# FOX heads of a hybrid attention block: weighing by three products of split operands, transposes in one row

## The chip, the cores and the metric

The kernel runs on one core of one Trainium2 chip. The metric is the device time of one execution in microseconds; three runs were taken and the median stands for the kernel.

## The reference, cut to what matters

One decoder layer in float32, 512 tokens, model width 2048: RMSNorm, one combined projection, native sparse attention (8 heads, the NSA part), forgetting attention (8 heads of 128, the FOX part), a gated merge of both, an output projection, and a feed-forward block with a depthwise convolution. The change touches the FOX part alone:

```python
def fox_attention(q, k, v, f_logit, f_bias):
    log_f = jax.nn.log_sigmoid(f_logit + f_bias)
    cum = lax.cumsum(log_f, axis=1).transpose(0, 2, 1)
    ...
    logits = einsum('bqhd,bkhd->bhqk', qblk, k) * scale + (cq[..., None] - cum[:, :, None, :])
    p = masked_softmax(logits, kpos[None, :] <= tpos[:, None])
    o = einsum('bhqk,bkhd->bqhd', p.astype(v.dtype), v)
```

## The kernel before, in words

Every engine has its own program written out by hand; semaphores order them. Large products are made of operands split into a high part rounded to fp32r and a low part that is the rest: `three` (its products are L809 to L811) issues high x high, high x low and low x high into one accumulation. Small products use plain float32, which the profile records as two passes.

The stage between the two halves of the merge holds the eight FOX heads, 0 to 7. TensorE's part of one head is `fox_step` on the tensor engine (L1175): scores of four query tiles (3, 2, 0, 1) into banks 2 to 4, split for all but tile 0; then products of a filler, `slot_cols`, which is one of the 22 plain blocks of the combined projection (16 steps `k` of three products of 512 columns, L809 to L811), there so that TensorE has work while the softmax of the head runs on VectorE (DVE) and ScalarE (ACT); then four transposes of V from `vf_fm` into bank 4 (L1187), ten transposes of the probabilities `l_fox` (L1085), the last filler step, and the weighing (`weigh`, L1091): O = V^T P^T with `vf_tm` as the stationary operand and `pt_f` as the moving one, for key tiles 0, 1, 3, 2 over 512, 384, 128 and 256 columns, into bank 7. The stage ends with one more filler block and `merge(S_BB, 1)`.

In each head DVE adds the bias and takes the maximum (L2207), splits the next filler's weights (`w_lo`, L1923), scales the probabilities (L2320), splits the next head's q and k (`fox_lo`, L2302), copies one bank of transposed probabilities to `pt_f` (L2326), and writes the filler's output (`plain_out`, L2152). ACT makes `w_hi` (L1361), issues the DMAs of the next head's `q_f` and `k_f` (L1645), takes the exponentials (L1564), rounds the next head's q and k (`fox_hi`, L1635), copies bank 4 to `vf_tm` (L1651), and banks of transposed probabilities to `pt_f` (L1653, L1655), and bank 7 to `y32` (L1657). Both run strictly in this order, so whatever waits for `q_f` and `k_f` holds up the copies behind it. SyncE (SP) issues per head, in this order: `vf_fm` of the next head (L675), the store of a filler's output (L593), `bias_f` (L679) and the weights of a later filler (`w_raw`, L499). POOL's queue meanwhile makes sums of feed-forward weights in DRAM.

## Time and profile before

| what | value |
|---|---|
| median of 3 runs | 2674.88 us (2674.46 to 2674.95) |
| profiled execution | 2675.92 us, its span 2674.1 us |
| FOX heads in the profile | scores of head 0 at about 940 us, weighing of head 7 to 1075.6 us |
| length of one head without a stall | 16.90 us |
| granted TensorE clock, mean | 0.995 |

PE is TensorE's matmuls, PEld its weight loads. A matmul's duration in the profile runs past the start of the next one, since they are pipelined: what an instruction costs is the distance from its start to the start of the next. SPq and ACTq are the issue of DMAs on those engines. Heads are counted from 0.

### The profile page before, as it was taken

To read this page: it belongs to the slowest core of one execution; us is meant where nothing else is said; L and a number is where in the kernel's file an instruction comes from. 1 tells how busy PE (TensorE), PEld (TensorE's weight loads), DVE (VectorE), ACT (ScalarE), POOL (GpSimd) and SP (SyncE) were. 2 spreads that over 40 slices of the span, in tenths; PEclk is the share of its full clock that TensorE was granted. 3 is DMA by queue.
4 is the path that set the end of the run, shared out by engine and by line. 5 is a ranking of instruction groups with operands and counts; after the bars stand their busy time and mean duration, and the time that the engine had idled before them with its cause. 6 is when DMAs were issued, how large, how long until landed. Compare 5 with 4: busy or idle time off the path is not lost.

```text
span 2674.1 us, 39866 instructions
## 1 busy us (share of the span) xinstructions
PE 2637.6 (99%) x14729; PEld 2280.2 (85%) x14729; DVE 2016.6 (75%) x2565; ACT 1227.7 (46%) x1618; POOL 497.4 (19%) x354
## 2 busy tenths in 40 slices
PE   8999999999999999999999999999999999999998
PEld 6899999987888877888888999999999998888886
DVE  5899899875554354542289999999999998888876
ACT  6444444434444244422355555555555544444445
POOL 0144444441442121220001111000000000000002
PEclk9999999999999999999999999999999999999999
DMA  7565666666666589779628888744354446666664
GB/s 224 148 194 176 196 181 177 200 191 172 158 165 177 175 248 254 236 242 247 183 87 212 208 193 208 157 126 122 106 133 114 107 114 234 223 229 224 221 210 151
DMA packets 499163, 489.54 MB, mean 183 GB/s; under 512 B 11589, under 2 KB 376790, under 8 KB 498281
## 3 DMA queue, kind: packets, MB, share of 16 engines
q1 hardware_dynamic: 454855, 367.14, 46.2%
q0 software_dynamic: 36112, 106.36, 16.5%
q10 hardware_dynamic: 8114, 14.95, 1.6%
q8 instruction: 50, 0.82, 0.1%
q14 instruction: 32, 0.26, 0.0%
HBM read 425.46 MB, written 127.96 MB: 207 GB/s over the span
## 4 chain that ended last, share of the span: by engine, by line
PE 92%; DMA 3%; DVE 2%; ACT 2%; issue 1%; SPq 0%; ACTq 0%; POOL 0%; DVEq 0%
PE bank L859 23%; PE bank L868 14%; PE bank L1343 14%; PE bank L861 12%; PE bank L809 8%; PE bank L811 8%; PE bank L810 8%; PE bank L1091 2%; PE bank L1085 1%; DMA k_f<-p_dram 1%; DMA w_raw<-in_w_in_dram 1%; DMA d_raw<-in_w_down_dram 1%; DVE ring_lo L2367 0%; DMA w_raw<-in_cmp_w_v_dram 0%; ACT sq_junk L1393 0%
## 5 line engine op out<-in xcount | busy, mean ns | idle before, releaser
L859 PE MATMUL bank<-hl,ring_hi 128*128 128x512 f32 x1032 | 368.4, 398 | 0.5 <-ACT v_sb L1735 0.5
L1343 PE MATMUL bank<-fold_hi,y_slot 128*128 128x512 f32 x1120 | 345.0, 389 | 0.0
L861 PE MATMUL bank<-hl,ring_lo 128*128 128x256 f32 x1032 | 289.8, 281 | 0.0
L1343 PEld LDWEIGHTS bank<-fold_hi,y_slot 128*128 128x128 f32 x1120 | 210.2, 188 | 43.8
L1923 DVE TENSOR_TENSOR w_lo<-w_raw,w_hi 128x2048 fp32r<-128x2048 f32 x59 | 135.9, 2303 | 145.6 <-ACT w_hi L1361 145.6
L1831 ACT ACTIVATE fold_hi<-x_raw 128x1024 fp32r<-128x1024 f32 x140 | 148.5, 1063 | 201.5 <-PE bank L1343 199.4
L859 PEld LDWEIGHTS bank<-hl,ring_hi 128*128 128x128 f32 x1032 | 194.0, 188 | 46.9 <-ACT v_sb L1735 0.7
L2771 POOL TENSOR_TENSOR v_sb<-v_sb,conv_t 128x512 f32<-128x512 f32 x44 | 68.3, 1552 | 881.2 <-ACT conv_t L1749 867.8
L1711 ACT ACTIVATE ring_hi<-s_a 128x1024 fp32r<-128x1024 f32 x129 | 137.0, 1062 | 202.7 <-PE bank L861 104.1
L1343 PE MATMUL bank<-fold_lo,y_slot 128*128 128x512 f32 x560 | 217.8, 389 | 0.0
L859 PE MATMUL bank<-hl,q_ring_hi 128*128 128x512 f32 x600 | 214.3, 399 | 2.3 <-issue 1.8
L861 PEld LDWEIGHTS bank<-hl,ring_lo 128*128 128x128 f32 x1032 | 195.1, 189 | 0.0
L2546 DVE TENSOR_TENSOR fold_lo<-x_raw,fold_hi 128x1024 fp32r<-128x1024 f32 x140 | 172.1, 1230 | 24.3 <-ACT fold_hi L1831 24.3
L809 PE MATMUL bank<-hl,w_hi 128*128 128x512 f32 x448 | 182.1, 407 | 6.4 <-DVE w_lo L1933 3.2
L1361 ACT ACTIVATE w_hi<-w_raw 128x2048 fp32r<-128x2048 f32 x59 | 113.0, 1915 | 163.5 <-PE bank L811 144.0
L811 PE MATMUL bank<-hl,w_lo 128*128 128x512 f32 x448 | 176.0, 393 | 0.0
L810 PE MATMUL bank<-hl,w_hi 128*128 128x512 f32 x448 | 175.8, 392 | 0.0
L861 PE MATMUL bank<-hl,q_ring_lo 128*128 128x256 f32 x600 | 168.5, 281 | 0.0
L2367 DVE TENSOR_TENSOR ring_lo<-raw,ring_hi 128x1024 fp32r<-128x1024 f32 x129 | 164.0, 1272 | 4.5 <-ACT ring_hi L1711 2.5
L2367 DVE TENSOR_TENSOR ring_lo<-s_a,ring_hi 128x1024 fp32r<-128x1024 f32 x129 | 157.5, 1221 | 5.3 <-ACT ring_hi L1711 5.1
L1423 ACT ACTIVATE q_ring_hi<-q_sum 128x1024 fp32r<-128x1024 f32 x75 | 79.6, 1061 | 161.5 <-DVE q_sum L2028 95.2
L1711 ACT ACTIVATE ring_hi<-raw 128x1024 fp32r<-128x1024 f32 x129 | 136.3, 1057 | 25.1 <-PE bank L868 23.8
(391 smaller groups left out, 7025.2 us busy)
## 6 DMA issues: line engine op xcount, KB each, us to landing
raw<-in_w_up_dram SPq DMA_DIRECT2D x43, 1024.0 KB, 7.2
raw<-in_w_up_dram SPq DMA_DIRECT2D x86, 512.0 KB, 7.5
w_s<-in_w_down_dram POOLq DMA_DIRECT2D x30, 1024.0 KB, 12.6
x_raw<-in_w_down_dram SPq DMA_DIRECT2D x30, 1024.0 KB, 5.1
w_raw<-in_w_in_dram SPq DMA_DIRECT2D x26, 1024.0 KB, 7.6
raw<-in_w_in_dram SPq DMA_DIRECT2D x25, 1024.0 KB, 8.6
raw<-in_w_in_dram SPq DMA_DIRECT2D x50, 512.0 KB, 7.2
x_raw<-w_s SPq DMA_DIRECT2D x20, 1024.0 KB, 5.4
```

The lines of the kernel that those rows point to most:

```text
L809: mm(dst, l_hi, r_hi, start=first, stop=False)
L810: mm(dst, l_hi, r_lo, start=False, stop=False)
L811: return mm(dst, l_lo, r_hi, start=False, stop=final)
L859: mm(pb[bank][:], hi[:, w], high_low(y[0][:, k, :], y[1][:, k, :]), start=first and k == 0, stop=False, skip_group_check=True)
L861: last = mm(pb[bank][:, 0:TH], lo[:, w], y[0][:, k, :], start=False, stop=k == KH - 1, skip_group_check=True)
L868: last = mm(pb[bank][:, 0:TH], left[:, w], y[z][:, k, :], start=first and k == 0 and n == 0, stop=k == KH - 1 and n == 2, skip_group_check ...
L1343: last = mm(pb[banks[tt]][:], y[:, z, k, tk], right[:, w], start=first and k == 0 and m == 0, stop=k == 3 and m == 2, skip_group_check=True)
L1711: A(ring_hi[b][:], src, ACT.Copy).then_inc(piece_hi, 1)
L1831: A(fold_hi[k % RING][:], x_raw[b][:, 1024 * h:1024 * h + 1024], ACT.Copy).then_inc(piece_hi, 1)
L1923: V.tensor_tensor(w_lo[:, s.par, :], w_raw[:, s.par, :], w_hi[:, s.par, :].bitcast(F32), ALU.subtract).then_inc(w_ready, 1)
L2367: V.tensor_tensor(ring_lo[b][:], src, ring_hi[b][:].bitcast(F32), ALU.subtract).then_inc(piece_ok, 1)
L2546: V.tensor_tensor(fold_lo[b][:], x_raw[FOLD_AT[p, n] % 4][:, 1024 * h:1024 * h + 1024], fold_hi[b][:].bitcast(F32), ALU.subtract).then_inc ...
```

## The change

The copies of V and of the transposed probabilities are rounded to fp32r (`vf_tm`, `pt_f`), and DVE makes their low parts: `vf_lo` from bank 4, `pt_lo0` from bank 5 (key tile 0, 512 columns), `pt_lo1` from bank 6 (tiles 1 and 3, 512 columns) and `pt_lo2` from bank 3 (tile 2, 256 columns). The weighing of each key tile is then `three` (products now at L812 to L814) in place of one plain product. The transposes of tile 2 go to bank 3, so that all ten stand in a row, and the filler's last three steps stand behind them in place of one between them and two ahead. `vf_lo` lies where `vf_fm` lies, so SP's load of the next head's V now waits for the end of the weighing (`fpv_done`) and no longer for the transposes of V (`fv_ps`).

```diff
--- before.py
+++ after.py
@@ -289,9 +289,12 @@
     kf_hi = at("kf_hi", A_ + 22 * KB, [P, SEQ], F32R)
     kf_lo = at("kf_lo", A_ + 24 * KB, [P, SEQ], F32R)
     vf_fm = at("vf_fm", A_ + 4 * KB, [P, SEQ])
-    vf_tm = at("vf_tm", A_ + 6 * KB, [P, TOK, P])
+    vf_lo = at("vf_lo", A_ + 4 * KB, [P, TOK, P], F32R)
+    vf_tm = at("vf_tm", A_ + 6 * KB, [P, TOK, P], F32R)
     l_fox = at("l_fox", A_ + 8 * KB, [P, 1280])
-    pt_f = at("pt_f", A_ + 13 * KB, [P, 1280])
+    pt_f = at("pt_f", A_ + 13 * KB, [P, 1280], F32R)
+    pt_lo = [at("pt_lo0", A_ + 26 * KB, [P, 512], F32R), at("pt_lo1", A_ + 32 * KB, [P, 512], F32R), at("pt_lo2", A_ + 34 * KB, [P, 256], F32R)]
+    PT_LO = {0: (0, 0), 1: (1, 0), 3: (1, 384), 2: (2, 0)}
     bias_f = at("bias_f", A_ + 36 * KB, [P, 2, SEQ])
 
     xr = at("xr", A_ + 32 * KB, [P, TOK, 512])
@@ -436,8 +439,8 @@
     f_hi_ok, f_lo_ok = sem("f_hi_ok"), sem("f_lo_ok")
     fs_ready, fs_read, fmax_ready, fexp_done, fr_ready, fp_ready = (
         sem(n) for n in ("fs_ready", "fs_read", "fmax_ready", "fexp_done", "fr_ready", "fp_ready"))
-    fv_ps, fv_ok, ft_ready, ft_act, ft_dve, fpv_done, fo_read = (
-        sem(n) for n in ("fv_ps", "fv_ok", "ft_ready", "ft_act", "ft_dve", "fpv_done", "fo_read"))
+    fv_ps, fv_ok, ft_ready, ft_act, fsplit_ok, fpv_done, fo_read = (
+        sem(n) for n in ("fv_ps", "fv_ok", "ft_ready", "ft_act", "fsplit_ok", "fpv_done", "fo_read"))
     mh_ok, ml_ok = sem("mh_ok"), sem("ml_ok")
     xr_loaded, wo_done, x1_add, x1_sq, x1_put, x1t_ps, x1t_read = (
         sem(n) for n in ("xr_loaded", "wo_done", "x1_add", "x1_sq", "x1_put", "x1t_ps", "x1t_read"))
@@ -671,7 +674,7 @@
 
         def load_fox_v(h):
             if h:
-                sp.wait_ge(fv_ps, h)
+                sp.wait_ge(fpv_done, h + 1)
             sp.dma_start(vf_fm[:], block_in(("VF", h))).then_inc(fv_in, 16)
 
         def load_bias_f(h):
@@ -1090,6 +1093,11 @@
 
             return mm(pb[7][:, j * P:SEQ], v[:, j, :], pt[:, PT_COL[j]:PT_COL[j] + SEQ - j * P], start=first, stop=final)
 
+        def weigh_split(j, first, final):
+
+            n, (b, c) = SEQ - j * P, PT_LO[j]
+            return three(pb[7][:, j * P:SEQ], vf_tm[:, j, :], vf_lo[:, j, :], pt_f[:, PT_COL[j]:PT_COL[j] + n], pt_lo[b][:, c:c + n], first, final)
+
         def nsa_step(s, g, filler):
             pe.wait_ge(q_in, s * 16 + 16)
             pe.wait_ge(o_done, s + 3)
@@ -1180,28 +1188,26 @@
                     pe.wait_ge(fv_ok, h + 1)
                 fox_scores(t).then_inc(fs_ready, 1)
             pe.wait_ge(o_done, h + 12)
-            slot_cols(s, s.par, range(0, KT - 1))
+            slot_cols(s, s.par, range(0, KT - 3))
             pe.wait_ge(fv_in, h * 16 + 16)
             pe.wait_ge(fs_read, h * 4 + 12)
             for j in range(TOK):
                 last = nc.tensor.transpose(pb[4][:, j * P:j * P + P], vf_fm[:, j * P:j * P + P], ident[:])
             last.then_inc(fv_ps, 1)
             pe.wait_ge(fp_ready, h + 1)
-            pe.wait_ge(ft_act, h * 2 + 2)
             transposes([0], 5, l_fox).then_inc(ft_ready, 1)
-            pe.wait_ge(ft_dve, h + 1)
             transposes([1, 3], 6, l_fox).then_inc(ft_ready, 1)
-            slot_cols(s, s.par, [KT - 1])
-            pe.wait_ge(ft_act, h * 2 + 3)
-            transposes([2], 5, l_fox).then_inc(ft_ready, 1)
+            transposes([2], 3, l_fox).then_inc(ft_ready, 1)
+            slot_cols(s, s.par, range(KT - 3, KT))
             pe.wait_ge(fo_read, h + 1)
-            pe.wait_ge(fv_ok, h + 2)
-            weigh(0, vf_tm, pt_f, True, False)
-            pe.wait_ge(ft_dve, h + 2)
-            weigh(1, vf_tm, pt_f, False, False)
-            weigh(3, vf_tm, pt_f, False, False)
-            pe.wait_ge(ft_act, h * 2 + 4)
-            weigh(2, vf_tm, pt_f, False, True).then_inc(fpv_done, 1)
+            pe.wait_ge(fsplit_ok, h * 5 + 1)
+            pe.wait_ge(fsplit_ok, h * 5 + 3)
+            weigh_split(0, True, False)
+            pe.wait_ge(fsplit_ok, h * 5 + 4)
+            weigh_split(1, False, False)
+            weigh_split(3, False, False)
+            pe.wait_ge(fsplit_ok, h * 5 + 5)
+            weigh_split(2, False, True).then_inc(fpv_done, 1)
 
         with pe.Fori(0, 3) as i:
             for b in range(2):
@@ -1652,7 +1658,7 @@
             act.wait_ge(ft_ready, h * 3 + 1)
             A(pt_f[:, 0:512], pb[5][:], ACT.Copy).then_inc(ft_act, 1)
             act.wait_ge(ft_ready, h * 3 + 3)
-            A(pt_f[:, 1024:1280], pb[5][:, 0:256], ACT.Copy).then_inc(ft_act, 1)
+            A(pt_f[:, 1024:1280], pb[3][:, 0:256], ACT.Copy).then_inc(ft_act, 1)
             act.wait_ge(fpv_done, h + 2)
             A(y32[:, ds(h, 1), :].rearrange("p a n -> p (a n)"), pb[7][:], ACT.Copy).then_inc(fo_read, 1)
 
@@ -2321,9 +2327,18 @@
             last.then_inc(fp_ready, 1)
             if more:
                 fox_lo(h + 1)
+            dve.wait_ge(fv_ok, h + 2)
+            dve.wait_ge(fpv_done, h + 1)
+            V.tensor_tensor(vf_lo[:].rearrange("p j d -> p (j d)"), pb[4][:], vf_tm[:].rearrange("p j d -> p (j d)").bitcast(F32),
+                            ALU.subtract).then_inc(fsplit_ok, 1)
             dve.wait_ge(ft_ready, h * 3 + 2)
-            dve.wait_ge(fpv_done, h + 1)
-            V.tensor_copy(pt_f[:, 512:1024], pb[6][:]).then_inc(ft_dve, 1)
+            V.tensor_copy(pt_f[:, 512:1024], pb[6][:]).then_inc(fsplit_ok, 1)
+            dve.wait_ge(ft_act, h * 2 + 3)
+            V.tensor_tensor(pt_lo[0][:], pb[5][:], pt_f[:, 0:512].bitcast(F32), ALU.subtract).then_inc(fsplit_ok, 1)
+            dve.wait_ge(fsplit_ok, h * 5 + 2)
+            V.tensor_tensor(pt_lo[1][:], pb[6][:], pt_f[:, 512:1024].bitcast(F32), ALU.subtract).then_inc(fsplit_ok, 1)
+            dve.wait_ge(ft_act, h * 2 + 4)
+            V.tensor_tensor(pt_lo[2][:], pb[3][:, 0:256], pt_f[:, 1024:1280].bitcast(F32), ALU.subtract).then_inc(fsplit_ok, 1)
             plain_out(1 - b, use + (b + 13) // 2, o_fox[:, 1 - b, :], done.par, done)
 
         with dve.Fori(0, 3) as i:
@@ -2676,7 +2691,7 @@
         pool.dma_start(fb[:], fox_forget_bias.rearrange("a h -> h a")).then_inc(wg_loaded, 16)
 
         for s_, n in ((ns_read, 18), (nt_ready, 6), (nt_dve, 1), (npv_done, 1), (br_read[0], 2), (br_read[1], 2),
-                      (fs_read, 8), (ft_dve, 1), (fpv_done, 1), 
+                      (fs_read, 8), (fpv_done, 1), 
                       (x1t_ps, 1), (x1_sq, 1), (x1_put, 16), (dn_add, 4), (halves_ok, 1), (a_out, 64), (p1_out, 1), (p5_out, 1), (u2_out, 1), (c11_out, 1), (c22_out, 1)):
             pool.sem_inc(s_, n)
```

TensorE, before, from the first transpose of probabilities of head 1 to the first weighing:

```order
L1085 MATMUL bank<-ident,l_fox 128x128 [waits ft_act,fp_ready]
L1085 MATMUL bank<-ident,l_fox 128x128 x3
L1085 MATMUL bank<-ident,l_fox 128x128 [waits ft_dve]
L1085 MATMUL bank<-ident,l_fox 128x128 x3
L809 MATMUL bank<-hl,w_hi 128x512
L810 MATMUL bank<-hl,w_hi 128x512
L811 MATMUL bank<-hl,w_lo 128x512
L1195 REGISTER_ALU
L1085 MATMUL bank<-ident,l_fox 128x128 [waits ft_act]
L1085 MATMUL bank<-ident,l_fox 128x128
L1198 REGISTER_ALU [waits fo_read]
L1091 MATMUL bank<-pt_f,vf_tm 128x512 [waits fv_ok]
```

and the same place now (the filler's three rows come three times):

```order
L1088 MATMUL bank<-ident,l_fox 128x128 [waits fp_ready]
L1088 MATMUL bank<-ident,l_fox 128x128 x9
L812 MATMUL bank<-hl,w_hi 128x512
L813 MATMUL bank<-hl,w_hi 128x512
L814 MATMUL bank<-hl,w_lo 128x512
...
L1203 ISA [waits fo_read]
L1204 REGISTER_ALU [waits fsplit_ok]
L812 MATMUL bank<-pt_f,vf_tm 128x512 [waits fsplit_ok]
L813 MATMUL bank<-pt_lo_110,vf_tm 128x512
L814 MATMUL bank<-pt_f,vf_lo 128x512
```

The ten transposes wait once, nine filler products stand between them and the weighing, and the weighing waits for DVE's splits. On DVE the same head, before, from the split of the next head's k to the next head's logits:

```order
L2302 TENSOR_TENSOR kf_lo<-k_f,kf_hi 128x512 [waits f_hi_ok]
L2324 ISA
L2326 COPY pt_f<-bank 128x512 [waits fpv_done,ft_ready]
L2149 REGISTER_ALU
L2151 ISA [waits w_used]
L2152 TENSOR_TENSOR o_fox<-bank,rbc 128x512 [waits o_put1]
L488 ISA [waits bf_loaded1]
```

and now:

```order
L2308 TENSOR_TENSOR kf_lo<-k_f,kf_hi 128x512 [waits f_hi_ok]
L2330 REGISTER_ALU
L2332 TENSOR_TENSOR vf_lo<-bank,vf_tm 128x512 [waits fpv_done,fv_ok]
L2334 ISA
L2335 CAST pt_f<-bank 128x512 [waits ft_ready]
L2336 ISA
L2337 TENSOR_TENSOR pt_lo_110<-bank,pt_f 128x512 [waits ft_act]
L2338 ISA
L2339 TENSOR_TENSOR pt_lo_111<-bank,pt_f 128x512 [waits fsplit_ok]
L2340 REGISTER_ALU
L2341 TENSOR_TENSOR pt_lo_112<-bank,pt_f 128x256 [waits ft_act]
L2155 REGISTER_ALU
```

Four splits stand around DVE's copy, behind the split of k and ahead of the filler's output.

## Rows read from the trace of the kernel before

**Rows 1.** The page's first part: busy time, share of the span and instructions.

```profile
PE 2637.6 (99%) x14729; PEld 2280.2 (85%) x14729; DVE 2016.6 (75%) x2565; ACT 1227.7 (46%) x1618; POOL 497.4 (19%) x354
```

**Rows 2.** The timeline of TensorE at 971.3 us; columns: start us, us, engine, line, operation.

```profile
971.44 2.32 PE L1091 MATMUL bank<-pt_f,vf_tm 128*128 128x512 f32 x8
...
973.83 0.39 PE L810 MATMUL bank<-kf_lo,qf_hi 128*128 128x512 f32 x1
974.06 0.40 PE L811 MATMUL bank<-kf_hi,qf_lo 128*128 128x512 f32 x1
...
974.60 0.34 PE L810 MATMUL bank<-kf_lo,qf_hi 128*128 128x384 f32 x1
974.77 0.33 PE L811 MATMUL bank<-kf_hi,qf_lo 128*128 128x384 f32 x1
...
975.52 0.28 PE L810 MATMUL bank<-kf_lo,qf_hi 128*128 128x256 f32 x1
975.64 0.28 PE L811 MATMUL bank<-kf_hi,qf_lo 128*128 128x256 f32 x1
```

**Rows 3.** The same view at 985.4 us.

```profile
986.11 0.60 PE L1187 MATMUL bank<-ident,vf_fm 128*128 128x128 f32 x4
986.55 1.04 PE L1085 MATMUL bank<-ident,l_fox 128*128 128x128 f32 x8
```

**Rows 4.** The timeline of all engines, 966.5 to 974 us; brackets: idle before, releaser.

```profile
968.42 0.60 PE L1187 MATMUL bank<-ident,vf_fm 128*128 128x128 f32 x4
...
968.99 0.63 ACT L1635 ACTIVATE qf_hi<-q_f 128x512 fp32r<-128x512 f32 x1 [6.28 <-DMA k_f<-p_dram]
969.05 0.33 SPq L675 DMA_DIRECT2D vf_fm<-p_dram  x1
...
970.87 0.68 DVE L2326 COPY pt_f<-bank 128x512 f32<-128x512 f32 x1
...
971.17 0.44 PE L1085 MATMUL bank<-ident,l_fox 128*128 128x128 f32 x2 [0.58 <-ACT pt_f L1653]
...
971.47 0.68 DVE L2152 TENSOR_TENSOR o_fox<-bank,rbc 128x512 f32<-128x512 f32 x1
```

**Rows 5.** The same view at 1000.2 us, head 3.

```profile
1000.35 0.63 ACT L1635 ACTIVATE qf_hi<-q_f 128x512 fp32r<-128x512 f32 x1 [3.08 <-DMA k_f<-p_dram]
```

**Rows 6.** The same view at 1018.4 us, head 4.

```profile
1018.52 0.63 ACT L1635 ACTIVATE qf_hi<-q_f 128x512 fp32r<-128x512 f32 x1 [4.03 <-DMA k_f<-p_dram]
```

**Rows 7.** The same view at 1035.1 us, head 5.

```profile
1035.24 0.63 ACT L1635 ACTIVATE qf_hi<-q_f 128x512 fp32r<-128x512 f32 x1 [4.04 <-DMA k_f<-p_dram]
...
1036.80 0.27 PE L1187 MATMUL bank<-ident,vf_fm 128*128 128x128 f32 x1
```

**Rows 8.** The same view at 1054 us, head 6.

```profile
1054.12 0.63 ACT L1635 ACTIVATE qf_hi<-q_f 128x512 fp32r<-128x512 f32 x1 [6.19 <-DMA k_f<-p_dram]
...
1056.30 0.44 PE L1085 MATMUL bank<-ident,l_fox 128*128 128x128 f32 x2 [0.43 <-ACT pt_f L1653]
```

**Rows 9.** The tile view of k_f, 934 to 1076 us, its last line.

```profile
DMA to landing us min/median/max: 3.5/6.8/9.1
```

**Rows 10.** The timeline of ACT, 973.5 to 991 us.

```profile
977.57 0.34 ACTq L1645 DMA_DIRECT2D q_f<-p_dram  x1
...
986.75 0.60 ACT L1651 ACTIVATE vf_tm<-bank 128x512 f32<-128x512 f32 x1 [3.56 <-PE bank L1187]
```

**Rows 11.** DMA queues, 959.5 to 969 us: packets, MB, share of 16 engines.

```profile
q0 software_dynamic: 677, 1.62, 74.2%
q1 hardware_dynamic: 942, 0.48, 21.1%
q10 hardware_dynamic: 288, 0.52, 14.6%
```

**Rows 12.** Windows at 587 us: length, busy by engine, PEclk, DMA share, GB/s.

```profile
590.70:594.10 3.40, 3.19 (x8) 2.54 (x9) 0.00 (x0) 1.91 (x1) 0.00 (x0) 0.50 1.15 330
```

**Rows 13.** The timeline of TensorE at 587 us.

```profile
590.91 0.77 PE L809 MATMUL bank<-hl,w_hi 128*128 128x512 f32 x1 [2.96 <-DMA hl<-y_dram]
```

## Prediction

> **What bounds the kernel now.** I read the page first: TensorE is busy 99% of the span, all others 75% or less [rows 1]. So whatever the change saves or adds on TensorE comes out at the end one to one, unless a wait takes it. Next I read TensorE's timeline through the FOX heads. The weighing starts at 971.44; the second product of the scores behind it starts at 973.83, and one product of 512 columns takes 0.23 us, so the weighing truly ends at 973.60 and costs 2.16 us [rows 2]. The filler follows without a gap in most heads. Two heads do stall. In head 1 the last two transposes wait 0.58 us for ACT's copy, in head 6 0.43 us [rows 4, 8]; with the 0.17 us by which a filler product's recorded end runs past its turn, the losses are 0.75 and 0.60 us. The timeline of all engines says why: ACT could begin the next head's qf_hi only when k_f had landed, at 968.99, after 6.28 us of waiting [rows 4], and at 1054.12 after 6.19 us [rows 8]. The copies of V and of the probabilities stand behind that on ACT, and on DVE behind the splits of q and k. So the FOX stage is bound by TensorE with a second limit close beneath: the landing of q_f and k_f, which takes 3.5 to 9.1 us from its issue [rows 9].
>
> **The weighing.** Removed: eight weighings of 2.16 us. Added: per head three products each of 512, 384, 128 and 256 columns. The scores give split products of the same kind: 512 columns 0.23 us (973.83 to 974.06), 384 columns 0.17 us (974.60 to 974.77), 256 columns 0.12 us (975.52 to 975.64) [rows 2]. None of 128 columns is in this trace. Its cost has bounds: by columns alone, half of 256, 0.06 us; and plain float32 at 128 columns, whose one pass is one of the transposes here, (986.55 - 986.11) / 4 = 0.11 us [rows 3], so 0.22 us for both passes. I take 0.12, the split product of 256 columns, since it is the nearest kind and a weight load of 128 columns has to fit into each turn in both. Sum: 3 x (0.23 + 0.17 + 0.12 + 0.12) = 1.92 us, which saves 0.24 us per head, **1.9 us in eight**. The bounds give savings of 3.4 us (0.06) and a loss of 0.5 us (0.22).
>
> The Trainium skill ("TensorE: Matmul & The Clock Gate", section "Back-to-back issue gap") gives about 81 ns for each pair of a weight load and a matmul of 128 columns. By that, an estimate from the page, the three would take 0.24 us in place of 0.36 and the sum would come out 1.0 us lower, at 2676.7; no row here has such a product at full rate.
>
> **The transposes.** They keep their number. Two waits on ACT and one on DVE between them go, worth nothing in the six heads without a stall. The filler keeps its 16 steps. But the first transpose of V now comes two steps earlier, 6 x 0.227 = 1.36 us. Its inputs are ready: l_fox is scaled several us ahead.
>
> **The new wait, and what stands in front of it.** From the first transpose of V TensorE has 14 transposes (14 x 0.109 = 1.53 us) and nine filler products (2.04 us) until the weighing, 3.57 us. The weighing needs DVE's third new step. Head 1 shows the chain, since there all waits for k_f: with A the start of qf_hi, DVE took its copy of pt_f at 970.87 = A + 1.88 and the next instruction 0.60 us later [rows 4]. Now vf_lo stands at A + 1.88, the copy at A + 2.48, the split of tile 0 at A + 3.08, done 0.69 us later; TensorE answers 0.05 us after that, A + 3.82. With T the old start of the transposes of V, TensorE would be there at T - 1.36 + 3.57 = T + 2.21. The stall is A - T + 1.61 where that is positive. The chain from T itself is no limit: vf_tm is written 986.75 + 0.60 - 986.11 = 1.24 us after the first transpose [rows 3, 10], and three DVE steps end 1.9 us later, 0.4 us ahead of TensorE. The later splits (0.60 us apart) end before the 0.69 and 0.85 us of products ahead of them are through.
>
> - Head 1: 968.99 - 968.42 = +0.57, stall 2.18 [rows 4].
> - Head 3: a head without a stall is 16.90 us long, so T is two of them before head 5's: 1000.35 - (1036.80 - 33.80) = -2.65, none, 1.04 to spare [rows 5, 7].
> - Head 4: 1018.52 - (1036.80 - 16.90) = -1.38, stall 0.23 [rows 6, 7].
> - Head 5: 1035.24 - 1036.80 = -1.56, stall 0.05 [rows 7].
> - Head 6: 1054.12 - (1036.80 + 16.90) = +0.42, stall 2.03 [rows 7, 8].
> - Heads 0, 2 have over 4 us to spare, head 7 loads nothing.
>
> Sum 4.5 us, of which 1.35 us was there: **3.1 us added**. In words: the copies have turned into a chain twice as long, and the filler behind the transposes covers it only when k_f is early.
>
> **SP's queue.** The load of V (L675) waited for the transposes of V and was issued at 969.05, 0.63 us after their start [rows 4]; now it waits for the end of the weighing, 3.57 + 1.92 + 0.2 = 5.7 us after the new start, so 3.7 us later. Queued behind it and later by the same: the filler's store, bias_f, and the weights w_raw. Each has a head or more until it is used, so their own lateness costs nothing; if that cover goes, it is w_raw of heads 2 and 7, which would hold ACT's w_hi and with it the exponentials. What matters is that 0.77 MB (three of 256 KB) now flow nearer to q_f and k_f. While these flowed in head 1, they had 0.52 MB in 288 packets, SP's queue only 0.48 MB in 942 small packets, w_raw's, and POOL's 1.62 MB [rows 11]: SP's three loads were over. Bounds of the shift of k_f: nothing or 1 us earlier in head 6, where they overlapped already; at most the whole 0.77 MB ahead of it at the (1.62 + 0.48 + 0.52) MB / 9.5 us = 0.28 MB/us of that stretch, 2.8 us later. I take 0.4 us in each of heads 1, 4, 5 and 6, near the lower end, since V's load now goes out at T + 4.3 and q_f at T + 8.4 (977.57 - 968.42, less the stall of 0.75) [rows 4, 10], so that SP's three should mostly be through: **1.6 us added**.
>
> **Sum.** -1.9 + 3.1 + 1.6 = +2.8 us on 2675.92, the profiled execution's own time, 2678.7. That execution stands 1.04 us above the median of the three runs; on the median it is 2677.7.
>
> **The rivals.**
>
> *Forecast (0.45).* As summed; its own range is 2674.6 (k_f not shifted, 128 columns at 0.06 us) to 2680.1 (k_f 1 us later in four heads).
>
> *Rival 1, slower (0.25): k_f lands later by over 1 us.* SP's three loads and q_f, k_f now share the engines. For it: in head 6 k_f took nearly the 9.1 us, with POOL's and SP's loads in the air. Against it: that lead of some 4 us. From about 1.0 us per head it decides: the result is then slower than before by 0.2%: -1.9 + 3.1 + 4.0 = +5.2. At 1.5 us it is +7.2, 2682.1; at the bound of 2.8 us four heads pay 11.2 and head 3 1.8, and the stall in heads 1 and 6 passes 4.8 us. This trace has an idle stretch of 2.96 us [rows 13] after which TensorE ran 3.4 us at a granted clock of 0.50, 1.2 GHz [rows 12]; at half clock that costs some 1.7 us each, in all +17.6, 2692.5.
>
> The Trainium skill ("DMA: Bandwidth & Descriptors", section "Queues, rings and completion order") says that each DMA engine takes turns between queues packet by packet. By that rule SP's large packets would get as many turns as q_f's where w_raw's small ones took little. By that rule the trace agrees: small packets moved few bytes each (0.5 KB against 1.8 KB) [rows 11]. It speaks for this rival.
>
> *Rival 2 (0.22): a split product of 128 columns costs as much as the plain one, 0.22 us.* Nothing in the trace excludes it: the kernel's split products all have 256 columns or more. The weighing then saves nothing (+0.06 per head), and the sum is 0.5 + 3.1 + 1.6 = +5.2, 2680.1.
>
> *Rival 3 (0.08): the stalls do not come.* With SP quiet at that time k_f lands early enough, also in heads 1 and 6: -1.9 - 1.35 = -3.3, 2671.6. With the cheapest products it is 2670.1. Against it: POOL's 1.62 MB are still there.
>
> **How the numbers follow.** 0.2% is 5.35 us, about what a measurement of this kernel can tell from no change. Faster by more would be under 2669.5, beyond rival 3 with its cheapest products: 0.02. Slower by more is over 2680.2: most of rival 1, half of rival 2 and a little of the forecast's upper edge, 0.30. The rest, 0.68, is within. The range runs from 2673.0, below the forecast's own edge and into rival 3, to 2686.0, which holds rival 2 and most of rival 1.
>
> **What would show it.** Right: products from pt_f and pt_lo with starts 0.23, 0.17, 0.12 and 0.12 us apart; TensorE idle ahead of the first of them in heads 1 and 6 by 2 to 3 us, released by DVE; k_f's landing with a median of about 7 us; unstalled heads 16.66 us long; SP's load of V issued at the end of the weighing. Wrong: 0.2 us between products of 128 columns (rival 2); stalls in heads 3, 4 and 5 of over 1 us (rival 1); no idle time at all ahead of the weighing (rival 3); a granted clock of 0.50 in the stage; or a stall in a head whose k_f was early, which would mean that DVE's chain is longer than I worked out.

## The result, and the profile after

| | before | changed |
|---|---|---|
| median, 6 runs each | 2674.91 us (2674.46 to 2675.99) | 2698.36 us (2695.47 to 2701.99) |
| profiled execution | 2675.92 us, span 2674.1 | 2698.33 us, span 2696.5 |

The ratio is 1.0089, 95% interval 1.0078 to 1.0099: the change makes the kernel **slower by 23.5 us**. The forecast was 2677.7 in a range of 2673.0 to 2686.0.

The page of the changed kernel, first part, answers to [rows 1]:

```profile
span 2696.5 us, 39980 instructions
...
PE 2643.6 (98%) x14761; PEld 2289.5 (85%) x14761; DVE 2031.4 (75%) x2597; ACT 1227.1 (46%) x1618; POOL 499.2 (19%) x354
```

TensorE's busy time rose by 6.0 us, the span by 22.4: most of it is waiting. Nearly all of it lies in the FOX heads. From the first transposes of V of head 0 to the merge behind the heads TensorE's timeline has 135.0 us before and 158.4 us now; less the 1.36 us by which those transposes stand earlier, this is +22.0. What stands ahead of them took 0.9 us more, what stands behind 0.5 us less.

**The weighing itself did what it should.** TensorE's timeline of the changed kernel at the end of head 0 (start us, us, engine, line, operation), which answers to [rows 2]:

```profile
954.68 0.39 PE L812 MATMUL bank<-pt_f,vf_tm 128*128 128x512 f32 x1
954.91 0.39 PE L813 MATMUL bank<-pt_lo,vf_tm 128*128 128x512 f32 x1
...
955.36 0.33 PE L812 MATMUL bank<-pt_f,vf_tm 128*128 128x384 f32 x1
955.53 0.34 PE L813 MATMUL bank<-pt_lo,vf_tm 128*128 128x384 f32 x1
...
955.89 0.23 PE L812 MATMUL bank<-pt_f,vf_tm 128*128 128x128 f32 x1
955.95 0.28 PE L813 MATMUL bank<-pt_lo,vf_tm 128*128 128x128 f32 x1
956.06 0.27 PE L814 MATMUL bank<-pt_f,vf_lo 128*128 128x128 f32 x1
956.17 0.34 PE L812 MATMUL bank<-pt_f,vf_tm 128*128 128x256 f32 x1
956.34 0.28 PE L813 MATMUL bank<-pt_lo,vf_tm 128*128 128x256 f32 x1
...
956.58 0.39 PE L812 MATMUL bank<-kf_hi,qf_hi 128*128 128x512 f32 x1
```

From the first product to the next head's scores it takes 956.58 - 954.68 = 1.90 us, against 2.16. The turns are 0.23 us at 512 columns, 0.17 at 384, at 128 columns 0.06 for the first (955.89 to 955.95) and 0.11 for the other two, and at 256 columns 0.17 for the first (956.17 to 956.34) and 0.12 for the other two. A head without a stall is 16.65 us long (16.90 before, 16.66 forecast).

**The waits.** The view of waits, 934 to 1099 us (engine, line, waited for: us in total, times, longest):

```profile
ACT qf_hi L1641 <- DMA k_f<-p_dram: 40.8, 7, 8.1
...
PE bank L812 <- DVE pt_lo L2337: 17.5, 5, 5.1
```

ACT waits 40.8 us for k_f (25.7 before). TensorE, which waited for no split before, stands idle five times ahead of the weighing, by 17.5 us as recorded. k_f's landing answers to [rows 9]:

```profile
DMA to landing us min/median/max: 3.4/9.6/11.6
```

The median went from 6.8 to 9.6 us. The windows from one head's first transpose to the next's, heads 0 to 6 (length, busy us with instructions by engine, granted clock, DMA share, GB/s):

```profile
951.09:967.74 16.65, 16.65 (x91) 14.03 (x90) 9.05 (x21) 6.17 (x13) 6.08 (x5) 1.00 0.71 167
967.74:987.28 19.54, 16.92 (x90) 13.95 (x89) 10.36 (x23) 8.49 (x16) 6.02 (x5) 1.00 0.89 293
987.28:1010.88 23.60, 18.98 (x91) 15.74 (x90) 10.26 (x23) 7.09 (x15) 5.50 (x4) 0.86 0.88 225
1010.88:1032.02 21.14, 18.42 (x90) 15.28 (x89) 10.36 (x23) 8.49 (x16) 5.49 (x4) 0.92 0.82 202
1032.02:1055.65 23.63, 18.49 (x91) 15.35 (x89) 11.09 (x23) 7.09 (x15) 5.70 (x4) 0.93 0.85 226
1055.65:1076.41 20.76, 18.38 (x90) 15.26 (x89) 10.26 (x23) 7.50 (x16) 2.76 (x3) 0.92 1.06 284
1076.41:1093.06 16.65, 16.65 (x90) 13.97 (x89) 10.26 (x23) 6.80 (x15) 1.19 (x1) 1.00 0.89 209
```

Heads 0 and 6 are whole at 16.65; heads 1 to 5 take 19.5 to 23.6 us, and in heads 2 to 5 the granted clock falls under 1. Head 2 shows how. DVE's timeline of the changed kernel there, with ACT's first row of the chain ahead of it; they answer to [rows 4]:

```profile
991.85 0.63 ACT L1641 ACTIVATE qf_hi<-q_f 128x512 fp32r<-128x512 f32 x1 [8.03 <-DMA k_f<-p_dram]
...
993.13 0.68 DVE L2308 TENSOR_TENSOR kf_lo<-k_f,kf_hi 128x512 fp32r<-128x512 f32 x1
...
993.73 0.68 DVE L2332 TENSOR_TENSOR vf_lo<-bank,vf_tm 128x512 fp32r<-128x512 f32 x1
...
994.33 0.68 DVE L2335 CAST pt_f<-bank 128x512 fp32r<-128x512 f32 x1
994.93 0.68 DVE L2337 TENSOR_TENSOR pt_lo<-bank,pt_f 128x512 fp32r<-128x512 f32 x1
```

and TensorE's:

```profile
995.66 0.79 PE L812 MATMUL bank<-pt_f,vf_tm 128*128 128x512 f32 x1 [4.62 <-DVE pt_lo L2337]
996.25 0.63 PE L813 MATMUL bank<-pt_lo,vf_tm 128*128 128x512 f32 x1
...
999.35 0.63 PE L812 MATMUL bank<-kf_hi,qf_hi 128*128 128x512 f32 x1
```

The chain is the forecast one: qf_hi at A = 991.85 once k_f is there, vf_lo at A + 1.88, the copy at A + 2.48, the split of tile 0 at A + 3.08, TensorE at A + 3.81. But TensorE had been idle for 4.78 us by then (its last filler product began at 990.65), and came back at the clock's lower level of 1.2 GHz (granted clock 0.50 from 995.7 to 999.3): 0.43 us for the turn of 512 columns (996.25 to 996.68), 3.69 us for the whole weighing (995.66 to 999.35) where 1.90 is full speed.

| head | k_f of the next head, issue to landing, before / now | stall, before / now | head's length now |
|---|---|---|---|
| 0 | 3.5 / 3.4 us | 0 / 0 us | 16.65 us |
| 1 | 8.9 / 9.6 | 0.75 / 2.78 | 19.55 |
| 2 | 3.9 / 11.6 | 0 / 4.78 | 23.59 |
| 3 | 5.7 / 9.7 | 0 / 2.88 | 21.15 |
| 4 | 7.0 / 11.3 | 0 / 5.29 | 23.63 |
| 5 | 6.8 / 9.3 | 0 / 2.54 | 20.77 |
| 6 | 9.1 / 6.9 | 0.60 / 0 | 16.65 |

The stalls sum to 18.27 us, 16.9 more than before. What the lengths of heads 1 to 5 hold above 16.65 and their stalls is 0.12, 2.16, 1.62, 1.69 and 1.58 us, together 7.2 us: time at half clock. With eight times 0.26 us saved: -2.1 + 16.9 + 7.2 = +22.0.

What was open after this: whether k_f came late because SP's loads now flow beside it (theory S), or because the first stall moved its issue against POOL's loads, which run by their own time (theory F).

### The profile page after: what moved, and what is told of

Its sections match the earlier page's. It is cut to its first block, busy times and chain, and to the rows that moved or that the text cites. A ratio compares the mean times of both kernels' runs of the same rounds, so it can differ in the third digit from the quotient of the medians.

```text
span 2696.5 us, 39980 instructions
## 1 busy us (share of the span) xinstructions
PE 2643.6 (98%) x14761; PEld 2289.5 (85%) x14761; DVE 2031.4 (75%) x2597; ACT 1227.1 (46%) x1618; POOL 499.2 (19%) x354
## 4 chain that ended last, share of the span: by engine, by line
PE 89%; DMA 4%; DVE 3%; ACT 2%; issue 1%; SPq 0%; ACTq 0%; POOL 0%; DVEq 0%
PE bank L862 22%; PE bank L871 14%; PE bank L1349 14%; PE bank L864 11%; PE bank L812 8%; PE bank L814 8%; PE bank L813 8%; DMA k_f<-p_dram 2%; PE bank L1094 1%; PE bank L1088 1%; DMA w_raw<-in_w_in_dram 1%; DMA d_raw<-in_w_down_dram 1%; DMA hl<-y_dram 0%; DVE ring_lo L2382 0%; DMA w_raw<-in_cmp_w_v_dram 0%
## 5 line engine op out<-in xcount | busy, mean ns | idle before, releaser
L812 PE MATMUL bank<-hl,w_hi 128*128 128x512 f32 x448 | 181.2, 404 | 6.2 <-DMA hl<-y_dram 3.1
L814 PE MATMUL bank<-hl,w_lo 128*128 128x512 f32 x448 | 176.1, 393 | 0.0
L1717 ACT ACTIVATE ring_hi<-raw 128x1024 fp32r<-128x1024 f32 x129 | 136.3, 1057 | 24.8 <-PE bank L871 23.5
```

The lines of the kernel that those rows point to most:

```text
L812: mm(dst, l_hi, r_hi, start=first, stop=False)
L814: return mm(dst, l_lo, r_hi, start=False, stop=final)
L1717: A(ring_hi[b][:], src, ACT.Copy).then_inc(piece_hi, 1)
```

## The experiments

The twelve were timed in three groups on two chips, each with the kernel before beside it; there its median was 2676.45, 2675.80 and 2675.64 us, single runs from 2670.6 to 2681.9. Every ratio is against the kernel before of the same group. So the profile's FOX stage is given beside each: **stage** is the time from head 0's first transpose of V to the merge, against 135.0 us in the kernel before, corrected by 1.36 us where the transposes stand earlier. It is that of one profiled execution, while the median is of four to eleven.

### Each half of the cause alone

**vf_lo in a place of its own.** The splits and the row of transposes stay, SP loads V on time.

```diff
-    vf_lo = at("vf_lo", A_ + 4 * KB, [P, TOK, P], F32R)
+    vf_lo = at("vf_lo", A_ + 40 * KB, [P, TOK, P], F32R)
...
-                sp.wait_ge(fpv_done, h + 1)
+                sp.wait_ge(fv_ps, h)
...
+        dve.wait_ge(o_put[1], 16 * 6)
```

The last line stands once ahead of the heads: `o_cover` lay in that place, and its store has to be over.

> The changed kernel with vf_lo in a place of its own, so that SP's load of V waits again for the transposes of V. All else as changed, the splits, the row of transposes and the filler behind. Theory S (SP's four loads, moved 3.7 us later, flow beside q_f and k_f and make k_f late): k_f lands 4 to 9 us after its issue as in the kernel before, stalls ahead of the weighing of about 2.2 and 2.0 us in heads 1 and 6 alone, no granted clock of 0.50 in the stage, time 2674.9 - 2.1 + 3.1 = about 2676. Theory F (the longer chain behind k_f alone is enough: the first stall moves the issue of q_f and k_f behind POOL's loads, and each stall makes the next): k_f still lands 9 to 11 us after its issue in heads 2 to 5, five stalls of 2.5 to 5 us, time 2690 or more.

Measured 2691.91 us (2677.68 to 2696.89 in ten runs), ratio 1.0046 (1.0027 to 1.0065); stage +18.8 us in the profiled run. So F is no small thing: with SP on time the longer chain loses 15.5 us by the medians, against 23.5 for the whole change. Four of the ten runs lie at 2678 to 2683 and six at 2691 to 2697: by their times the loss starts in some executions and not in others; one of the six was profiled. How it starts there is in the timeline of head 2, here of this kernel:

```profile
973.58 0.54 POOL L2732 DMA_DIRECT2D w_s<-w_n  x1
...
974.08 0.34 ACTq L1651 DMA_DIRECT2D q_f<-p_dram  x1
974.10 1.17 POOL L2733 DMA_DIRECT2D w_s<-in_w_down_dram  x1
...
974.59 0.46 ACTq L1651 DMA_DIRECT2D k_f<-p_dram  x1
```

and of the kernel before:

```profile
977.66 0.78 POOL L2707 DMA_DIRECT2D w_n<-nb_late  x1 [0.30 <-POOL nb_late L2705]
...
978.07 0.34 ACTq L1645 DMA_DIRECT2D k_f<-p_dram  x1
...
978.44 0.54 POOL L2716 DMA_DIRECT2D w_s<-w_n  x1
...
978.96 1.17 POOL L2717 DMA_DIRECT2D w_s<-in_w_down_dram  x1
```

Before, k_f went out 0.37 us ahead of POOL's first sum and landed after 3.9 us. Here q_f and k_f went out 0.50 and 1.01 us behind it, and k_f took 11.3 us, which made a stall of 4.5 us in head 2, and another of 4.3 us in head 3: a cascade, in which each stall makes the next. It has two halves. Without head 1's stall of 1.5 us k_f would have gone out 0.5 us ahead of the sum (an estimate from these rows). But the kernel before had a stall of 0.75 us there too, and q_f went out 26.0 us behind the place of head 0's transposes of V in both (the 1.36 us taken off here); POOL's sum went out 1.4 us sooner here, since the load of nb_late ahead of it landed after 9.7 us and not after 11.3.

**SP late alone.** The kernel before with one wait changed.

```diff
-                sp.wait_ge(fv_ps, h)
+                sp.wait_ge(fpv_done, h + 1)
```

> The kernel before with SP's load of V waiting for the end of the weighing, and nothing else. Theory S: k_f lands 9 to 11 us after its issue in heads 2 to 5; the old, shorter chain makes stalls of some 1.2 to 3.4 us in heads 1 to 5, 9 us more than before in sum, time about 2684, more if the clock falls. Theory F: landings as before, time 2675 to 2676.

Measured 2695.13 us (2691.32 to 2697.64), ratio 1.0067 (1.0049 to 1.0085), stage +19.8 us. k_f's tile view:

```profile
DMA to landing us min/median/max: 3.6/9.7/12.9
```

S holds and was sized too low: this one wait, under plain weighing and the old order, costs 18.7 us by the medians (of four runs here), where some 9 were expected. Each half alone loses most of what both lose together, so their costs don't add up. TensorE waits for ACT's copy ahead of the last transposes:

```profile
PE bank L1085 <- ACT pt_f L1653: 14.0, 6, 4.6
```

**The row of transposes alone.** The kernel before with ten transposes in a row and three filler steps behind, plain weighing.

```diff
-            slot_cols(s, s.par, range(0, KT - 1))
+            slot_cols(s, s.par, range(0, KT - 3))
...
+            transposes([2], 3, l_fox).then_inc(ft_ready, 1)
+            slot_cols(s, s.par, range(KT - 3, KT))
             pe.wait_ge(fo_read, h + 1)
             pe.wait_ge(fv_ok, h + 2)
+            pe.wait_ge(ft_act, h * 2 + 3)
             weigh(0, vf_tm, pt_f, True, False)
```

> The kernel before with the ten transposes in a row, tile 2's to bank 3, and three filler steps behind them; plain weighing, no splits, SP as before. The chain behind k_f ends 2.56 us after it lands (DVE's copy), TensorE asks for it 2.21 us after the old start of the transposes of V less what the first copy allows: stalls of about 0.5 and 0.4 us in heads 1 and 6 in place of 0.75 and 0.60. Both theories: 2674.4, the same as before. If the row itself costs (clock, banks), over 2677.

Measured 2677.03 us, ratio 1.0004 (0.9995 to 1.0014): no difference. Its profiled run had a stage of +2.6 us, from one stall in head 6:

```profile
1060.41 1.10 PE L1091 MATMUL bank<-pt_f,vf_tm 128*128 128x512 f32 x2 [2.71 <-ACT pt_f L1651]
```

There k_f took 9.8 us. The row itself costs nothing that these runs show; it shares the old weakness.

### The traffic taken away

**POOL's sums behind the FOX heads.** The changed kernel; the eight sums of DRAM blocks go to the loop behind.

```diff
-            sums_in_dram(2 + h // 4, h % 4)
...
-        for k in range(8):
-            sums_in_dram(4 + k // 4, k % 4)
+        for k in range(16):
+            sums_in_dram(2 + k // 4, k % 4)
```

> The changed kernel with POOL's eight sums in DRAM (1 to 2 MB per head) taken out of the FOX heads and made behind them; the same work, later. Both theories need POOL's traffic: k_f should land in 3 to 6 us in all heads, no stall over 0.5 us, the weighing's saving of 0.26 us per head comes out and the two old stalls go: 2674.9 - 2.1 - 1.35 = about 2671.5, if the later sums are in time. If SP's own shift is enough by itself (S in its strong form), k_f stays at 7 us and over and the time above 2678.

Measured 2678.78 us (2674.84 to 2683.72), ratio 1.0006 (0.9997 to 1.0016); stage +0.2 us, k_f:

```profile
DMA to landing us min/median/max: 3.0/7.1/7.6
```

Without POOL's sums SP's late loads alone hold k_f at 7.1 us in the median, steadily: four stalls of 0.3 to 1.4 us, and no cascade. The forecast of 3 to 6 us was wrong, its strong alternative for S right on k_f. That the time is above 2678 us too is no merit of S: in the profiled run the heads lost 0.2 us, the part behind them 5.9. The moved sums cost at the first feed-forward block, where the profile names no releaser:

```profile
1359.86 0.77 PE L812 MATMUL bank<-hl,w_hi 128*128 128x512 f32 x1 [4.83 <-issue]
```

**The same with vf_lo in its own place.**

> The changed kernel with vf_lo in its own place, SP on time, and POOL's eight sums behind the FOX heads; the copies still behind k_f. If SP's and POOL's traffic together make k_f late, k_f now lands in 3 to 5 us in every head, no stall ahead of the weighing, 3.4 us under the kernel before; with SP late and the sums out of the way k_f had taken 7 us. If another cause holds k_f up, it stays at 7 us.

Measured 2677.43 us, ratio 1.0008 (0.9998 to 1.0017). In the stage it does all that was forecast, -3.4 us, every head 16.66 us long, with k_f at

```profile
DMA to landing us min/median/max: 2.8/3.3/3.8
```

and 4.1 us are lost at the same later place, so that the forecast of 3.4 us under the kernel before fails for the whole. With SP's late loads and POOL's sums both out of the way no head is left in which k_f is late.

**The sums spread.** Eight sums behind FOX, the rest in 24 feed-forward units in place of 16, once with the changed kernel (vf_lo in its own place), once with the kernel before.

```diff
-            sums_in_dram(2 + h // 4, h % 4)
...
-            sums_in_dram(4 + k // 4, k % 4)
+            sums_in_dram(2 + k // 4, k % 4)
...
-            if n < 16:
-                sums_in_dram(6 + n // 4, n % 4)
+            if n < 24:
+                sums_in_dram(4 + n // 4, n % 4)
```

> The changed kernel with vf_lo in its own place, POOL's eight sums out of the FOX heads as before, but no more than 8 sums between FOX and the feed-forward part; the rest go into 24 feed-forward units in place of 16. The FOX stage stays at 116.9 us as with the sums out, and the 4 to 7 us that the output projection had lost to 16 sums behind FOX do not appear: 3.4 us under the kernel before. Rival: they do appear, since any sum there is in the way, or the feed-forward part pays.

> The kernel before with POOL's sums spread in the same way: its two stalls of 0.75 and 0.60 us go, heads of 16.90 us, 1.35 us under the kernel before. The run above should be 2.0 us faster than this one: that is the weighing by three products by itself.

Measured 2672.99 us, ratio 0.9992 (0.9983 to 1.0001), and 2674.06 us, ratio 0.9993 (0.9984 to 1.0002). Stages: -3.5 and -1.4 us, no loss behind. By the stages the weighing by three products is worth 2.0 us, as forecast for it; by the medians the two differ by 1.1 us, less than either interval is wide, so that the timed runs don't settle its size. k_f of the first:

```profile
DMA to landing us min/median/max: 2.8/3.1/4.2
```

### The chain taken away

**The next head's q and k split behind the copies.** On ACT `fox_hi(h + 1)` moves behind the copies of V and the probabilities, on DVE `fox_lo(h + 1)` behind the splits; SP late as in the change.

```diff
             exps(l_fox, 4).then_inc(fexp_done, 1)
-            if more:
-                fox_hi(h + 1)
...
             A(pt_f[:, 1024:1280], pb[3][:, 0:256], ACT.Copy).then_inc(ft_act, 1)
+            if more:
+                fox_hi(h + 1)
...
+            if more:
+                fox_lo(h + 1)
             plain_out(1 - b, use + (b + 13) // 2, o_fox[:, 1 - b, :], done.par, done)
```

> The changed kernel with fox_hi (on ACT) and fox_lo (on DVE) of the next head moved behind the copies and splits of V and of the probabilities; SP late as in the change. If the whole loss comes from the copies standing behind k_f, the weighing no longer waits for k_f, which may then come 1.96 us before the next head's scores, some 3.5 us after the first transpose of V: head 1's +2.6 us fits, so the first stall and with it all later ones go. No granted clock of 0.50 in the stage, all heads 16.65 us long, time 2.1 + 1.35 = 3.4 us under the kernel before of the same chip. If k_f's lateness (10 us and over) did not come from the first stall but from SP's place alone, heads 2 and 4 (+4.6, +4.3 us) would still stall by about 1 us ahead of the scores, and the time is about the kernel before's.

Measured 2674.03 us (2672.98 to 2677.03), ratio 0.9995 (0.9986 to 1.0004): the 23 us are gone with no transfer made smaller. Stage -2.1 us. k_f still took 10.0 us in head 1 and 11.3 us in head 2, then 5.9 to 8.6: SP's place makes k_f late without any stall ahead of the weighing, and in the changed kernel the stalls keep it late. The one stall left is head 2's, the 1 us named for it:

```profile
993.46 0.49 PE L812 MATMUL bank<-kf_hi,qf_hi 128*128 128x512 f32 x1 [0.97 <-DVE kf_lo L2308]
```

**The same with SP on time.**

> The same with vf_lo in its own place and SP on time. k_f 4 to 9 us after its issue as in the kernel before, no stall in any head, 3.4 us under the kernel before. Were SP's place a cost of its own even without stalls, this one would be faster than the run with SP late.

Measured 2673.66 us, ratio 0.9993 (0.9984 to 1.0002), stage -1.9 us. TensorE waits for k_f nowhere; one stall was not foreseen, in head 6, ahead of the transposes of probabilities, which were scaled late:

```profile
1050.56 0.44 PE L1088 MATMUL bank<-ident,l_fox 128*128 128x128 f32 x2 [1.17 <-DVE l_fox L2327]
```

It comes back in the last of the runs below, where its cause is shown.

**The kernel before with the same move.**

> The kernel before with the same move of fox_hi and fox_lo alone: its stalls of 0.75 and 0.60 us in heads 1 and 6 go, heads 16.90 us long, 1.35 us faster than before, which is under what a measurement tells from no change. If the weighing by three products saves nothing, this run and the one above are equal.

A miss: 2678.10 us, ratio 1.0010 (1.0000 to 1.0019), stage +1.9 us, every head 17.33 to 17.40 us long. In the old order ACT's last copy comes late in the head, so the splits behind it are late for the next scores in every head:

```profile
956.46 0.49 PE L809 MATMUL bank<-kf_hi,qf_hi 128*128 128x512 f32 x1 [0.24 <-DVE kf_lo L2302]
```

The move pays only with the transposes in one row, which the change brought.

### The order of issue

**POOL held until k_f has landed**, with vf_lo in its own place; then the same with the split of q and k behind.

```diff
             pool.wait_ge(fr_ready, h + 1)
+            if h < HEADS - 1:
+                pool.wait_ge(fqk_in, (h + 2) * 32)
```

> The changed kernel with vf_lo in its own place and SP on time, and in each head POOL starts its loads and sums only when the next head's k_f has landed; the amount is the same, the copies still stand behind k_f. Theory F says that the order of issue decides: in the run with vf_lo in its own place alone, POOL's sums went out 0.5 us ahead of q_f in head 2 and k_f took 11.3 us, where before they went out 0.9 us behind it and k_f took 3.9 us. Held back, k_f should take 4 to 7 us in every head, no stall ahead of the weighing passes 1 us and none makes the next, FOX stage 116.6 to 119 us from the first to the last transposes of V (before 120.1, that run 139.1), time 1 to 3.4 us under the kernel before. Rival: it is the sum of bytes and not their order; then k_f stays at 8 to 11 us, with stalls as there.

Measured 2679.51 us (2676.35 to 2682.87), ratio 1.0015 (1.0006 to 1.0024), stage +5.0 us. Half right. No stall makes the next: behind the stall of head 1 k_f lands in 2.7 us in head 2. But k_f took 8.5 us in heads 1, 4 and 6, under sums issued a head earlier and still in flight, with stalls of 1.7 to 2.5 us where at most 1 was expected. So the hold ends the cascade, and what is in flight already makes the single stall.

> The same with fox_hi and fox_lo of the next head behind the copies and splits as well. Both limits on k_f are off: all heads 16.66 us long, the stage from the first to the last transposes of V 116.7 us, 3.4 us under the kernel before. The one stall of 1.4 us that the run without the hold still had in head 6, ahead of the transposes of probabilities, goes too if it came from late filler weights under POOL's traffic.

Measured 2672.91 us (2667.77 to 2675.62), **ratio 0.9988 (0.9979 to 0.9997)**, the one version whose interval lies wholly under the kernel before. That does not show it to be the best of them: its profiled stage is -1.5 us only, where the one with the sums spread has -3.5, and the intervals overlap. Heads 0 to 5 are 16.67 us long. The stall in head 6 did not go (0.9 us as recorded, TensorE waiting for the scaled probabilities). ACT's timeline shows why:

```profile
1047.31 1.92 ACT L1367 ACTIVATE w_hi<-w_raw 128x2048 fp32r<-128x2048 f32 x1 [6.13 <-DMA w_n<-nb_late]
```

Ahead of head 6 ACT's program has a wait of its own for POOL's store of nb_late (`nb_io`), and everything in ACT's head stands behind it, q_f and k_f too. That store went out at 1041.01 and landed after 6.3 us, w_hi began 0.02 us later, and the split of the weights, the scaling and the transposes came late in turn. The run without the hold has the same row, with 6.34 us of idle time. So the late weights that the expectation named come from this wait, and not from the load of w_raw, which had landed at 1028.1.

**Head 2 in eight of the kernels** (from their timelines; w_raw is the fourth load of SP, 1 MB, issued behind V, the store and bias_f):

| run | w_raw issued ahead of q_f | k_f issued, against POOL's first sum | k_f's landing |
|---|---|---|---|
| kernel before | 7.1 us | 0.4 us ahead | 3.9 us |
| SP on time, q and k split behind | 7.7 | 0.4 ahead | 3.9 |
| SP late, q and k split behind | 2.3 | 0.4 ahead | 11.3 |
| SP on time, sums behind FOX | 7.1 | no sums | 2.8 |
| SP late, sums behind FOX | 1.6 | no sums | 7.1 |
| vf_lo in its own place | 8.7 | 1.0 behind | 11.3 |
| SP late alone | 2.0 | 3.3 behind | 12.9 |
| changed kernel | 2.0 | 2.6 behind | 11.6 |

The second and third rows have the same order of q_f, k_f and POOL's sums and differ by SP's place: k_f 3.9 and 11.3 us. So the order against POOL is only half of it. The rows of the third:

```profile
977.25 0.41 SPq L502 DMA_DIRECT2D w_raw<-in_w_in_dram  x1
...
979.56 0.34 ACTq L1651 DMA_DIRECT2D q_f<-p_dram  x1
980.07 0.53 ACTq L1651 DMA_DIRECT2D k_f<-p_dram  x1
...
980.43 0.55 POOL L2731 DMA_DIRECT2D w_s<-w_n  x1
```

With SP late and no sums k_f landed within 0.6 us of w_raw in each of heads 1 to 6 (in head 2 both at 985.9), while SP's three small loads of head 2 landed at 978.2, 979.0 and 980.8, the last of them 2.5 us behind q_f's issue. That points at w_raw; no run moved it alone.

## Why the prediction was wrong, point by point

- **What bounds the kernel: right.** TensorE, with the landing of q_f and k_f close beneath. The landing was taken as a fixed time, though.
- **The weighing, 1.92 us: right** at 1.90, in part by luck: the three products of 128 columns took 0.28 us where 0.36 was taken, those of 256 columns 0.41 where 0.36 was taken. Rival 2 fell. The 81 ns for a pair of 128 columns that the Trainium skill gives ("TensorE: Matmul & The Clock Gate", section "Back-to-back issue gap") lies between the 60 and 110 ns measured.
- **The chain, A + 3.82 and stall = A - T + 1.61: right.** With the landings as they came it gives 2.8, 4.8, 2.9, 4.5 and 2.6 us for heads 1 to 5; measured 2.78, 4.78, 2.88, 5.29 and 2.54. Head 4's extra 0.8 us is below.
- **The landings taken from the trace before, "3.1 us added": wrong in kind.** They were put in as fixed offsets from each head's start. They follow from what else is in flight at the issue, and the stall of one head moves the next head's issue against POOL, whose sums follow their own loads. Head 2 was given "over 4 us to spare" and had the second longest stall. The run with SP on time has none of SP's shift and still loses 18.8 us in the stage.
- **SP's queue, "1.6 us added": the term that failed first.** 0.4 us per head was taken and 2.8 us called the bound; k_f came 0.7, 7.7, 4.0, 4.3 and 2.5 us later in heads 1 to 5. The bound counted SP's 0.77 MB alone, at the 0.28 MB/us of one stretch. It left out two things. SP's fourth load, the 1 MB of w_raw, moves with the three: of all four the prediction says that "their own lateness costs nothing", and what w_raw does to k_f it put at nothing. At the same 0.28 MB/us it is 3.7 us, an estimate, and with the sums out of the way SP's place makes k_f 3.8 us later in the median (7.1 against 3.3). Of the three small loads V and the store were through by q_f's issue, or within 0.2 us of it, in heads 2 and 3 of the changed kernel, but not in heads 1 and 5. And a stalled head issues q_f behind POOL's next 1 to 2 MB. This wait alone costs 18.7 us by the medians of its group.
- **Rival 1 was the right rival at the wrong size.** Its mechanism, k_f later by over 1 us with half clock at its end, is what happened. But it shifted every head by a fixed time and knew no cascade. It was priced to 17.6 us at the utmost and given 0.25, and the half clock was counted for two heads, not four.
- **SP's late loads cost nothing by themselves: right**, V, the store, bias_f and w_raw were waited for by nobody in the changed kernel's heads; what they cost is to k_f.

The Trainium skill's rule of turns between queues ("DMA: Bandwidth & Descriptors", section "Queues, rings and completion order") spoke for rival 1, and the runs agree in direction: with the sums taken away and SP put back on time k_f goes from 9.6 to 3.3 us in the median. None of these runs shows the turns themselves.

## What to carry to other kernels

Ask of each wait that is added to a DMA queue what will then be in flight together, counting all that stands behind it in the queue, the largest load above all, and of each stage with little slack whether a stall moves its own next transfer behind another queue's: a delay that feeds itself costs many times its first size. Take work that waits for a far transfer out of the way of work that doesn't, before adding to the latter: the same change with the splits of q and k behind the copies gave back all 23 us, although k_f still took up to 11.3. A landing time read from one trace is a draw, not a constant; ask how far it can move.

## What the runs showed that was not expected

The granted clock fell to 0.50 after idle times of 2.54 to 5.29 us in heads 2 to 5 but not after 2.78 us in head 1, nor after 2.87 us in the run with the row of transposes alone; each fall cost 1.6 to 2.2 us. Earlier only a stretch of 2.96 us had shown it [rows 12, 13].

DVE's split of k took 1.52 us in head 4 in place of 0.68, and pushed the weighing by 0.8 us (DVE's timeline of the changed kernel, then POOL's):

```profile
1036.93 0.69 DVE L2308 TENSOR_TENSOR qf_lo<-q_f,qf_hi 128x512 fp32r<-128x512 f32 x1 [7.21 <-ACT qf_hi L1641]
1037.54 1.52 DVE L2308 TENSOR_TENSOR kf_lo<-k_f,kf_hi 128x512 fp32r<-128x512 f32 x1
1038.99 0.68 DVE L2332 TENSOR_TENSOR vf_lo<-bank,vf_tm 128x512 fp32r<-128x512 f32 x1
```

```profile
1037.15 3.10 POOL L2720 TENSOR_SCALAR nb_late<-nb_late 128x1024 f32<-128x1024 f32 x1 [7.67 <-DMA nb_late<-in_w_down_dram]
```

The split of q, begun ahead of POOL's scaling of nb_late, took 0.69 us; the split of k, begun within it, 1.52 us; the split of V, which has an input in PSUM, 0.68 us although POOL was still working. The same 1.52 to 1.53 us stand in three other runs, for splits of k that began 0.1 to 0.4 us into POOL's scaling; splits of k that began 1.5 us or more into it kept to 0.69 us at most. The Trainium skill ("SBUF — State Buffer", section "SBUF: two separate sides") says that a tensor_tensor of VectorE with both inputs in SBUF contends with GpSimd's reads, and that the loser blocks for the whole instruction. The trace agrees on which form is slowed, not on the second part: the split of k ended at 1039.06, POOL's instruction at 1040.25, though spans on POOL are rough. No run took POOL's scaling away alone, so the cause is read from these rows and not tested.

The kernel before spread over 11 us on one chip of the experiments, over 7 us on the other and over 1.5 us where it was first timed. In the traces head 0's transposes of V begin between 946.7 and 953.5 us with nearly the same code ahead of them, so that part of the spread lies ahead of the stage. That is why differences of 1 to 3 us were read from the stage and not from medians.
